# Streamed fp32 weights split into high and low parts: a ring of four halves in place of two full steps

## The reference, cut to what matters

```python
for layer in range(DEPTH):
    mp = adaln(c_prompt, w_ada[layer], b_ada[layer])      # silu(c) @ w_ada, 2048 x 12288
    hp = modulate(yp, g_mix[layer], mp[0], mp[1])
    ... mixers on hp @ w_in_ab (layer 0) or hp @ w_in_cd (layer 1) ...
    yp = yp + mp[2][:, None, :] * (op @ w_out[layer])
    yp = swiglu_sublayer(yp, mp[3], mp[4], mp[5], g_ffn[layer], w_ffn_gate[layer],
                         w_ffn_up[layer], w_ffn_down[layer])
```

## Time and profile before

| | us |
|---|---|
| median of 3 runs (3020.37 to 3024.21) | 3024.14 |
| span of the profiled execution | 3025.1 |
| PE busy in it | 2829.3 (94%) |
| DVE busy | 1414.4 (47%) |
| ACT busy | 1177.5 (39%) |
| mean DMA rate, 602.59 MB | 199 GB/s |

### The profile page before, as it was taken

One profiled execution on the slowest core, in us unless ns is written; L12 is line 12 of the kernel. 1 busy time (PEld: TensorE's weight loads), 2 busy tenths in 40 slices (PEclk: granted clock), 3 DMA queues, 4 the chain that ended last, 5 costly groups with the idle time before them and its releaser, 6 DMA issues.

```text
span 3025.1 us, 50764 instructions
## 1 busy us (share of the span) xinstructions
PE 2829.3 (94%) x20229; PEld 2570.6 (85%) x20229; DVE 1414.4 (47%) x2017; ACT 1177.5 (39%) x1508; POOL 79.0 (3%) x108
## 2 busy tenths in 40 slices
PE   5699995898999999999999899889899999999997
PEld 1488884687888888888999899669799999999997
DVE  0399945434443433344444535534545544444443
ACT  1333344234444332333443435433444433444433
POOL 1000000010000000000000000001000000000000
PEclk7699996599999999999999999669999999999999
DMA  9767757375777677877534444114344434444343
GB/s 383 254 259 270 279 223 84 118 273 203 272 272 283 255 281 307 318 266 272 206 132 171 151 164 158 50 60 154 125 166 166 158 135 179 167 166 166 141 155 124
DMA packets 83601, 602.59 MB, mean 199 GB/s; under 512 B 29301, under 2 KB 30645, under 8 KB 31938
## 3 DMA queue, kind: packets, MB, share of 16 engines
q1 hardware_dynamic: 83522, 601.54, 54.4%
HBM read 592.01 MB, written 9.49 MB: 199 GB/s over the span
## 4 chain that ended last, share of the span: by engine, by line
PE 85%; DVE 4%; ACT 4%; DMA 3%; issue 3%; SPq 1%; DVEq 0%; POOL 0%; ACTq 0%; POOLq 0%
PE ps L556 25%; PE ps L557 24%; PE ps L558 24%; PE ps L572 5%; DMA raw<-in_w_ada 3%; DVE w_lo L1191 1%; DVE cacc L1280 1%; ACT tn L1013 1%; PE ps L702 1%; PE ps L582 1%; ACT w_hi L868 1%; PE ps L741 1%; SPq L413 1%; ACT act_hi L1020 1%; PE ps L721 0%
## 5 line engine op out<-in xcount | busy, mean ns | idle before, releaser
L1191 DVE TENSOR_TENSOR w_lo<-raw,w_hi 128x2048 fp32r<-128x2048 f32 (+2 forms) x404 | 838.1, 2075 | 1172.4 <-ACT w_hi L868 1160.5
L556 PE MATMUL ps<-act_hi,w_hi 128*128 128x288 f32 x4400 | 1323.6, 301 | 64.4 <-DVE act_lo L1363 40.7
L557 PE MATMUL ps<-act_hi,w_lo 128*128 128x288 f32 x4400 | 1304.1, 296 | 0.0
L558 PE MATMUL ps<-act_lo,w_hi 128*128 128x288 f32 x4400 | 1299.0, 295 | 0.0
L868 ACT ACTIVATE w_hi<-raw 128x2048 fp32r<-128x2048 f32 (+2 forms) x404 | 702.2, 1739 | 1123.7 <-PE ps L558 1120.7
L556 PEld LDWEIGHTS ps<-act_hi,w_hi 128*128 128x128 f32 x4400 | 830.3, 189 | 154.3 <-issue 117.3
L558 PEld LDWEIGHTS ps<-act_lo,w_hi 128*128 128x128 f32 x4400 | 834.3, 190 | 0.0
L557 PEld LDWEIGHTS ps<-act_hi,w_lo 128*128 128x128 f32 x4400 | 832.3, 189 | 0.0
L556 PE MATMUL ps<-hid_hi,w_hi 128*128 128x288 f32 x1408 | 421.6, 299 | 8.5 <-DVE w_lo L1191 8.5
L558 PE MATMUL ps<-hid_lo,w_hi 128*128 128x288 f32 x1408 | 419.8, 298 | 0.0
L557 PE MATMUL ps<-hid_hi,w_lo 128*128 128x288 f32 x1408 | 419.8, 298 | 0.0
(11 more groups left out here) (239 smaller groups left out, 1357.1 us busy)
## 6 DMA issues: line engine op xcount, KB each, us to landing
raw<-in_w_gu SPq DMA_DIRECT2D x88, 2048.0 KB, 7.7
aring<-in_w_ada SPq DMA_DIRECT2D x160, 1024.0 KB, 7.0
raw<-in_w_dn SPq DMA_DIRECT2D x64, 1408.0 KB, 6.0
raw<-in_w_ab SPq DMA_DIRECT2D x20, 2048.0 KB, 7.8
raw<-in_w_ada SPq DMA_DIRECT2D x32, 1024.0 KB, 8.3
raw<-in_w_out SPq DMA_DIRECT2D x16, 2048.0 KB, 7.9
raw<-in_w_cd SPq DMA_DIRECT2D x13, 2048.0 KB, 7.8
aring<-in_state_glaT SPq DMA_DIRECT2D x4, 1024.0 KB, 9.9
```

The source lines that it names most:

```text
L556: pe.matmul(bank, w_hi[:, h, cols], hi[:, kt, :], start=begin, stop=False)
L557: pe.matmul(bank, w_lo[:, h, cols], hi[:, kt, :], start=False, stop=False)
L558: mm = pe.matmul(bank, w_hi[:, h, cols], lo[:, kt, :], start=False, stop=end)
L1191: dve.tensor_tensor(w_lo[:, h, 0:w], raw[:, par, h * w:(h + 1) * w], w_hi[:, h, 0:w].bitcast(F32), ALU.subtract).then_inc(split_done, 1)
```

## The change

Loading, splitting and freeing go by halves. `raw` keeps its size, and `w_lo` now has the same place as `raw`: DVE writes each low part over the half that it came from. `w_hi` is doubled to the freed size, with a place for each parity and half. Four semaphores, one for each place, tell that a half has landed. ACT no longer waits for `half_done` before it splits. SP now loads half h of step n when PE has finished half h of step n-2 (`half_done` at 2n + h - 3). The first step's halves wait for slots 1 and 2 of unit 7 (`ada_used` at 4*PRE - 2 + h).

```diff
-        raw = sb("raw", [P, 2, SLOT])
-        w_hi = sb("w_hi", [P, 2, SLOT // 2], F32R)
-        w_lo = sb("w_lo", [P, 2, SLOT // 2], F32R)
+        with ExitStack() as a:
+            raw = sb("raw", [P, 2, SLOT], stack=a)
+        with ExitStack() as a:
+            w_lo = sb("w_lo", [P, 2, SLOT], F32R, stack=a)
+        sb("weights", [P, 2, SLOT])
+        w_hi = sb("w_hi", [P, 2, SLOT], F32R)
...
+            def load_half(seg, n, par, ls, h):
+
+                if not (isinstance(n, int) and n < 2):
+                    sp.wait_ge(half_done, n * 2 + (h - 3))
+                w = seg.width // 2
+                rows = src[seg.kind][bass.ds(ls + (seg.first + seg.layer * LAYER_STEPS.get(seg.kind, 0)), 1)]
+                sp.dma_start(raw[:, par, h * HALF:h * HALF + w], rows[:, :, h * w:(h + 1) * w].rearrange("a p n -> p (a n)")) \
+                    .then_inc(weights_landed[2 * par + h], 16)
+
             def load_step(seg, n, par, ls):
 
-                if not (isinstance(n, int) and n < 2):
-                    sp.wait_ge(split_done, n * 2 - 2)
-                rows = src[seg.kind][bass.ds(ls + (seg.first + seg.layer * LAYER_STEPS.get(seg.kind, 0)), 1)]
-                sp.dma_start(raw[:, par, 0:seg.width], rows.rearrange("a p n -> p (a n)")) \
-                    .then_inc(weights_landed[par], 16)
+                for h in range(2):
+                    load_half(seg, n, par, ls, h)
...
-            sp.wait_ge(ada_used, 4 * PRE - 3)
-            load_step(SEGS[0], 0, 0, 0)
+            for h in range(2):
+                sp.wait_ge(ada_used, 4 * PRE - 2 + h)
+                load_half(SEGS[0], 0, 0, 0, h)
...
-                    pe.matmul(bank, w_hi[:, h, cols], hi[:, kt, :], start=begin, stop=False)
+                    pe.matmul(bank, w_hi[:, par, cols], hi[:, kt, :], start=begin, stop=False)
...
             def split(seg, n, par, h):
 
-                act.wait_ge(weights_landed[par], (n - par) * 8 + 16)
-                if not (isinstance(n, int) and n == 0):
-                    act.wait_ge(half_done, n * 2 + (h - 1))
-                w = seg.width // 2
-                act.activation(w_hi[:, h, 0:w], raw[:, par, h * w:(h + 1) * w], ACT.Copy).then_inc(hi_done, 1)
+                act.wait_ge(weights_landed[2 * par + h], (n - par) * 8 + 16)
+                half_w = slice(h * HALF, h * HALF + seg.width // 2)
+                act.activation(w_hi[:, par, half_w], raw[:, par, half_w], ACT.Copy).then_inc(hi_done, 1)
```

More of the change, by code:

```diff
@@ L42 @@
 SLOT = 2 * KT * P
+HALF = SLOT // 2
 ADA_N = 512
@@ L270, in build @@
         la = ps[:, 7, P:P + T]
-        weights_landed = [sem("weights_landed0"), sem("weights_landed1")]
+        weights_landed = [sem(f"weights_landed{q}") for q in range(4)]
         ada_landed = [sem("ada_landed0"), sem("ada_landed1")]
@@ L552, in half @@
                         pe.wait_ge(hid_ready, hidden + kt + 1)
-                    cols = slice(k * P, (k + 1) * P)
+                    cols = slice(h * HALF + k * P, h * HALF + (k + 1) * P)
                     begin = k == 0 and (seg.two or h == 0)
                     end = k == seg.ktiles - 1 and (seg.two or h == 1)
-                    pe.matmul(bank, w_hi[:, h, cols], hi[:, kt, :], start=begin, stop=False)
-                    pe.matmul(bank, w_lo[:, h, cols], hi[:, kt, :], start=False, stop=False)
-                    mm = pe.matmul(bank, w_hi[:, h, cols], lo[:, kt, :], start=False, stop=end)
+                    pe.matmul(bank, w_hi[:, par, cols], hi[:, kt, :], start=begin, stop=False)
+                    pe.matmul(bank, w_lo[:, par, cols], hi[:, kt, :], start=False, stop=False)
+                    mm = pe.matmul(bank, w_hi[:, par, cols], lo[:, kt, :], start=False, stop=end)
                 mm.then_inc(half_done, 1)
@@ L1189, in split_lo @@
                 dve.wait_ge(hi_done, n * 2 + (h + 1))
-                w = seg.width // 2
-                dve.tensor_tensor(w_lo[:, h, 0:w], raw[:, par, h * w:(h + 1) * w], w_hi[:, h, 0:w].bitcast(F32),
+                half_w = slice(h * HALF, h * HALF + seg.width // 2)
+                dve.tensor_tensor(w_lo[:, par, half_w], raw[:, par, half_w], w_hi[:, par, half_w].bitcast(F32),
                                   ALU.subtract).then_inc(split_done, 1)
```

## The result

The changed kernel takes 3153.29 us (median of 4 runs, 3150.96 to 3159.11) against 3024.18 for the kernel before, a ratio of 1.0435 with a 95% interval of 1.0422 to 1.0448. The profiled execution's span went from 3025.1 to 3149.3 us, by 124.2.

The account below looks back on a forecast made before the run. PE, busy 94% of the span, was taken as the bound. Slots 106 + 45, mix0 6.5, less 3.1 and 1.8, make +153; with +51 for the clock, 3025.1 becomes 3229, median 3228 us; range 3150 to 3290.

Parts of the forecast that it names:

- rival 1: Whole kernel: the waits come but the clock stays at 2.4 GHz, 3178 us, or 3177 for the median; 20%.
- What bounds the kernel: Long segments: matmuls on PE alone set the time; ACT's 1120.7 us of waiting before its splits is slack.
- Slots behind the half: Modulation units: slots issued behind a just-freed half land late, +106 us in 32 units and +45 us in down.
- The 0.3 us for SP: SP's queue: estimated time from the start of PE's next instruction to SP's issue.
- The price of each further 1024 KB: SP's loads: 4.9 us for the first 1024 KB on an empty queue, 3.0 us for each further one.
- The row of 4096 KB: Loads issued from 592.38 to 594.10, all landed 13.8 us after the first issue; source of the 3.0 us.
- The page: Trainium skill's figures set against the forecast: 4.4 us for 1024 KB, 2.4 for each more, giving 3085 us.
- The clock: Modulation units: a fall after slot 3 in three of four, 40 x 0.75 x 1.7 = +51 us; bounds 0 and 82.
- three cases at 2.6 us: Starts of down segments: the clock falls behind all three gaps of this size, costing 1.7 us.
- mix0: Stores of the convolution's state, issued 9.5 us later behind the last z half: PE +6.5 us, bounds 4 and 9.5.
- What it gives: Gate segment: four waits for w_lo, 3.1 us in all, go because ACT splits earlier.
- The 12 us at the start of gate and those at the starts of down: Waits for w_lo claimed to stay: 12.0 us at 133.36, and 8.5 us at the four starts of down.

Follow-up runs that it names:

- slots_between: Changed kernel, with SP issuing a step's two slots between the loads of the first and second half: 3017.32 us, ratio 0.9993.
- before_wait_pe: Kernel before, with SP waiting ahead of a step's two slots until PE has finished the step before: 3031.12 us, ratio 1.0043.
- joined_gap: Changed kernel, with PE waiting for slot 3 to land before it starts slot 2: 3208.93 us, ratio 1.0624.
- whole_steps: Changed kernel, with each step loaded in one transfer, issued when PE has freed the second half: 3492.83 us, ratio 1.1566.
- before_halves: Kernel before, with each step loaded in two transfers issued back to back under the same wait: 3021.16 us, ratio 1.0001.

## Why the prediction was right, and which terms were off

The time, 3153, lies in the range (3150 to 3290) near its lower end; the forecast was 3228. Of the cases, rival 1 (3177, the waits without the clock) came nearest. The mechanism was right; that the range held is luck in part. Of 204 us forecast 129 were measured, the waits for slots and the clock were both put too high, and the time lies 3 us inside the lower bound. Some 8 us that the sum had no term for (the last point below) put it there.

- **What bounds the kernel.** Right: ACT's 1120.7 us before the splits were slack. They fell to 138.2 (before ACT's splits, for PE) and the waits for w_lo fell by 3.7 us. The ring gives PE nothing where PE is busy anyway.
- **Slots behind the half.** Right in mechanism, and shown from three sides: away from that place they cost nothing (slots_between), with nothing ahead of them a tenth (before_wait_pe), with twice as much 2.6 times as much waiting (286.5 against 109.8 us). The 0.3 us for SP were 0.24, and the half issued at 990.20 landed after 4.9 us, as in the earlier trace rows.
- **The price of each further 1024 KB.** This term was mis-sized. The working took 3.0 us from four pieces issued over 1.7 us; here slot 3 follows slot 2 by 2.43 us, and slot 2 has landed 7.5 us after the half's issue where 7.9 were expected. The error counts twice at slot 3, which has two pieces ahead: a wide unit lost 2.4 us in place of 3.5, a down unit 4.1 in place of 5.65. 151 us were worked out for all units; 108 were measured. The row of 4096 KB was no clean case: the second piece landed 3.9 us behind the first, and the last 2048 KB 5.0 us behind the second, which is 2.5 for each 1024 KB. SP's second issue lasts 1.3 us there, and a further slot was issued at 601.94, before the last piece landed. Which of these made the mean of 3.0 is not shown; it was a bound from above and was taken as the value.
- **The page.** The Trainium skill, DMA: Bandwidth & Descriptors, section "Anatomy of one DMA — SWDGE (gpsimd) path", has 2.0 us and the bytes at 436 GB/s for the GpSimd path, so, as an estimate, 4.4 us for the first 1024 KB and 2.4 for each more. The measured 2.43 agrees with its slope, the measured 4.9 doesn't agree with its start. With 4.9 and the measured 2.43 the working gives 1.7 us for a wide unit and 4.6 for a down unit, 89 us in all against the 108 measured: nearer than 151, and too low, since in the first segments PE waited longer (4.8 us in the unit at 278 to 299 us).
- **The clock.** The step that failed: 51 us forecast, from a fall in 30 of 40 units. In the trace the clock falls at slots 2 and 3 in 6 units, for 24 us in all, so at most 12 us of cost. Over the whole span the low time rose by 378 - (1 - 0.939) x 3025 / 0.5 = 9 us only, at most 4 to 5 us of cost, since falls of the kernel before at other places are gone. It went wrong twice. The gaps were 1.4 us and not 2.0, since the landing was mis-sized; and the slot between two gaps was taken as nearly nothing for the clock. In the changed kernel 1.1 and 1.4 us on both sides of a slot leave it at 2.4 GHz in most units. Joined to 2.5 us and more they bring it down in 22 units (joined_gap), and two gaps of some 2.8 and 1.4 us bring it down nearly always (whole_steps). The prediction had three cases at 2.6 us and read them as a rule for two gaps with work between. The rule does not even hold for the same three gaps: in the changed kernel the clock falls behind one of them, at 2565.85, and stays at 2.4 GHz behind the two at 1714.27 and 2993.73.

```profile
2565.00:2570.00 5.00, 4.15 (x20) 4.16 (x21) 3.86 (x3) 1.67 (x2) 0.00 (x0) 0.66 0.29 115
1714.00:1719.00 5.00, 4.73 (x35) 4.73 (x36) 3.29 (x3) 1.10 (x1) 0.00 (x0) 1.00 0.23 91
2993.00:2998.00 5.00, 4.27 (x32) 4.27 (x33) 3.74 (x3) 1.56 (x2) 0.00 (x0) 1.00 0.31 124
```

- **mix0.** +6.5 forecast, +7.7 measured in the wait, one trace against another (the same wait is 19.7 us in before_wait_pe and 20.7 in before_halves, which leave the stores as they were, so a few us are scatter). In the changed kernel SP's stores, the turn of unit 17 and PE's go stand as follows, as the earlier trace rows:

```profile
478.91 0.95 PE L593 MATMUL ps<-sel,adarow 128*128 128x9 f32 x8
...
479.47 0.61 SPq L421 DMA_DIRECT2D out_conv_p<-uext  x1
480.12 21.95 SPq L423 DMA_DIRECT2D out_conv_s<-uext  x8
...
515.48 0.66 PE L662 MATMUL ps<-ident,free_lo 128*128 128x128 f32 x2 [30.49 <-ACT vtok_s L1060]
```

  The stores now start 1.2 us behind the turn, where they were 8.2 ahead of it: 9.4 us, as the 9.5 of the working; from the first store to PE's go it is 35.4 us (480.12 to 515.48) where it was 38.3, about what 1024 KB less ahead would give.
- **What it gives.** -3.1 at w_lo: measured -3.7. The 12 us at the start of gate and those at the starts of down stayed, as said.
- **What the sum had no term for.** Waits for aring 108.0, mix0 7.7, w_lo -3.7 and the clock's 4 to 5 make 116 to 117 of the 124.2 us. The other 7 or 8 are not idle time, since PE's busy time rose by 14.7 us, and 12.0 of it lies in the slots (163.0 to 175.0 on the pages). Slots 2 and 3 in one piece take 1.92 us; with a gap between them they take 1.06 each, 0.2 more, since the second no longer starts before the first has ended. In the 39 units with such a gap that is 8 us. This is worked out from the rows; no run isolates it.

## What to carry to other kernels

On a queue that issues in order, a load's wait is also the wait of everything behind it, and a load issued at that moment is a transfer time ahead of everything behind it; so after each change of what a load waits for, walk down the queue and price the next user of each place. A place that only the last consumer frees is loaded later, however many places the ring has: put loads with less slack between the early and the late half. Idle time on ACT or DVE that PE's work covers is no reserve; the same ring paid only once the splits moved out of the chain at the ends of segments.

## What the runs showed of the hardware

A transfer of 1024 KB on SP's queue landed 4.9 us after issue with nothing ahead of it, and the two issued right behind it followed by 2.6 and 2.43 us (the unit in gu shown above). Splitting 2048 KB in two transfers cost nothing (1.0001). In the changed kernel, where most units have a gap of up to 2.1 us, 1 us of narrow matmuls and a gap of 1.4 us in a row, TensorE's clock stayed at 2.4 GHz there in 34 of 40 units. It went either way behind single gaps of 2.5 to 3.9 us: three times of three at 2.6 us in the kernel before, once of three in the changed one, in 22 of 40 units in joined_gap. Where gaps of some 3 us came with each unit (whole_steps) it spent 384 us more of the span at 1.2 GHz.
